# Turning attention weights with partition moves and VectorE in place of TensorE, in a one-core encoder block

## The reference

```python
# differential attention, 8 heads: 64-wide q and k in two maps, 128-wide v, 64-token chunks, block-causal
p = softmax(where(mask, q @ k.T * 64**-0.5, -inf))      # (8 heads, 2 maps, 256, 256)
a = p[:, :, 0] - lam * p[:, :, 1]
o = rmsnorm(a @ v, g_diff_sub) * (1.0 - lambda_init)    # per head, then @ w_diff_out

# cross attention into 256 memory tokens, 4 heads of width 256
s = (q @ k.T) * 256**-0.5
o = softmax(s) @ v                                      # then @ w_cross_out
merged = g_a * y_conv + g_b * y_diff + g_c * y_cross
```

## Time and profile before

| what | value |
|---|---|
| median of 3 runs | 1661.82 us (1661.12 to 1662.33) |
| the profiled execution's own time | 1663.99 us |
| its span in the trace | 1662.2 us |
| TensorE's granted clock, mean of the span | 0.999 of full speed |
| PE busy | 1648.3 us, 99% of the span, 7397 instructions |
| DVE busy | 991.1 us, 60%, 1259 instructions |
| ACT busy | 832.6 us, 50%, 1062 instructions |
| POOL busy | 23.6 us, 1% |
| DMA moved | 338.78 MB, mean 204 GB/s |

### The profile page before, as it was taken

The page is one execution under the profiler, slowest core; times in us unless marked ns, Lnnn a source line. Parts: engine busy times, 40 slices in busy tenths (PEclk is TensorE's granted clock), DMA queues, the critical chain, the costliest instruction groups (busy, mean ns, idle before and its releaser), DMA issues.

```text
span 1662.2 us, 22134 instructions
## 1 busy us (share of the span) xinstructions
PE 1648.3 (99%) x7397; PEld 1361.0 (82%) x7397; DVE 991.1 (60%) x1259; ACT 832.6 (50%) x1062; POOL 23.6 (1%) x53
## 2 busy tenths in 40 slices
PE   8999999999999999999999999999999999999998
PEld 7888888888888888888888888888888888888886
DVE  5555556655556656656555657676667767744544
ACT  5544444444444444444445556656666565543442
POOL 0000000000000000000000000000000000000000
PEclk9999999999999999999999999999999999999999
DMA  7677666777556655566556477777777777755653
GB/s 273 204 207 207 183 177 183 228 215 221 186 184 199 229 189 183 184 228 196 195 188 215 143 213 216 221 213 222 216 215 226 209 210 225 241 191 172 218 190 139
DMA packets 191907, 338.78 MB, mean 204 GB/s; under 512 B 19224, under 2 KB 37481, under 8 KB 191337
## 3 DMA queue, kind: packets, MB, share of 16 engines
q1 hardware_dynamic: 191817, 338.01, 64.9%
q10 hardware_dynamic: 32, 0.01, 0.0%
HBM read 318.02 MB, written 2.10 MB: 193 GB/s over the span
## 4 chain that ended last, share of the span: by engine, by line
PE 97%; DVE 1%; ACT 1%; issue 1%; DMA 0%; DVEq 0%; SPq 0%; POOL 0%; ACTq 0%; POOLq 0%
PE PS L1267 28%; PE PS L1269 28%; PE PS L1268 27%; PE PS L1414 3%; PE PS L1413 3%; PE PS L1412 3%; PE PS L1448 1%; PE PS L1447 1%; PE PS L1446 1%; PE PS L1281 1%; ACT w_hi L499 0%; PE PS L1353 0%; PE PS L1338 0%; DMA mem_sb<-in_mem_dram 0%; ACT p_diff L635 0%
## 5 line engine op out<-in xcount | busy, mean ns | idle before, releaser
L834 DVE TENSOR_TENSOR w_lo<-raw,w_hi 128x1024 fp32r<-128x1024 f32 x567 | 691.0, 1225 | 608.0 <-ACT w_hi L499 606.4
L499 ACT ACTIVATE w_hi<-raw 128x1024 fp32r<-128x1024 f32 x567 | 597.5, 1059 | 656.3 <-PE PS L1269 603.1
L1267 PE MATMUL PS<-w_hi,hT_hi 128*128 128x512 f32 x1504 | 590.0, 392 | 0.0
L1269 PE MATMUL PS<-w_hi,hT_lo 128*128 128x512 f32 x1504 | 585.6, 389 | 0.0
L1268 PE MATMUL PS<-w_lo,hT_hi 128*128 128x512 f32 x1504 | 585.3, 389 | 0.0
L1267 PEld LDWEIGHTS PS<-w_hi,hT_hi 128*128 128x128 f32 x1504 | 282.4, 188 | 60.4 <-issue 2.7
L1269 PEld LDWEIGHTS PS<-w_hi,hT_lo 128*128 128x128 f32 x1504 | 282.3, 188 | 58.9
L1268 PEld LDWEIGHTS PS<-w_lo,hT_hi 128*128 128x128 f32 x1504 | 282.5, 188 | 57.7
L1267 PE MATMUL PS<-w_hi,act_hi 128*128 128x512 f32 x336 | 130.9, 389 | 0.0
L1269 PE MATMUL PS<-w_hi,act_lo 128*128 128x512 f32 x336 | 130.7, 389 | 0.0
L1268 PE MATMUL PS<-w_lo,act_hi 128*128 128x512 f32 x336 | 130.7, 389 | 0.0
(11 more groups left out here) (217 smaller groups left out, 1269.7 us busy)
## 6 DMA issues: line engine op xcount, KB each, us to landing
raw<-in_w_up_dram SPq DMA_DIRECT2D x176, 512.0 KB, 4.0
raw<-in_w_in_dram SPq DMA_DIRECT2D x112, 512.0 KB, 4.1
raw<-in_w_gate_dram SPq DMA_DIRECT2D x96, 512.0 KB, 4.2
raw<-in_w_down_dram SPq DMA_DIRECT2D x88, 512.0 KB, 4.2
raw<-in_w_mem_kv_dram SPq DMA_DIRECT2D x32, 512.0 KB, 4.0
raw<-in_w_o_dram SPq DMA_DIRECT2D x32, 512.0 KB, 3.6
up_moved<-up_stage SPq DMA_DIRECT2D x352, 32.0 KB, 2.8
raw<-in_w_conv_out_dram SPq DMA_DIRECT2D x16, 512.0 KB, 3.7
```

The lines of the kernel that those rows point to most:

```text
L499: nc.scalar.activation(w_hi[i % RING][:], raw[i % RING][:], ACT.Copy).then_inc(hi_ready, inc)
L834: nc.vector.tensor_tensor(w_lo[i % RING][:], raw[i % RING][:], w_hi[i % RING][:].bitcast(F32), ALU.subtract).then_inc(lo_ready, inc)
L1267: nc.tensor.matmul(o, a_hi, b_hi, start=first, stop=False)
L1269: last = nc.tensor.matmul(o, a_lo, b_hi, start=False, stop=last_k)
```

## The change

- **Cross heads.** PE's four turns and ACT's copy are gone. DVE normalizes into `p_stage` in 32-wide squares (four instructions in place of two). SP moves the squares to `p_moved` with 16 DMAs of 32 partitions by 512 bytes, four behind each of the loads 4 to 7 of chunk `c = h + 8`. DVE turns them in four instructions behind its block 4 of that chunk. PE multiplies with the values behind block 2 of it, one chunk later than before, into another PSUM bank; ACT and DVE split the result behind 6.
- **Differential heads, weights.** PE's three turns and ACT's copy are gone. DVE writes `a_stage` in squares (three instructions in place of two). SP moves them to `a_moved` with 16 DMAs of 32 partitions by 384 bytes: behind loads 10 and 11 of the step and loads 0 and 1 of the next. DVE turns them in three instructions behind block 11, before the gate's argument. PE multiplies behind block 9 in place of 4. ACT's squares move behind block 0 of the next step, DVE's scaling behind its block 2.
- **Differential heads, outputs.** PE's two turns per head are gone. DVE scales into `o_stage`. Once for four heads, in step j = 0 of r = 1 and of r = 2, SP moves them with 16 DMAs of 32 partitions by 1 KB behind loads 6 to 9, DVE turns them in four instructions behind block 7, and ACT and DVE split four heads at once behind 8.
- **POOL.** The copy of the next head's q and k now comes ahead of the norm of the last head.

```diff
+        a_stage = at("a_stage", RD + 71 * K, [P, P // SQ, 3, SQ])
+        a_moved = at("a_moved", RD + 72 * K + 512, [P, P // SQ, 3, SQ])
+        a_diffT = at("a_diffT", RD + 74 * K, [P, 3 * P])
+        p_stage = at("p_stage", RD + 72 * K, [P, P // SQ, 2 * NT, SQ])
+        p_moved = at("p_moved", RD + 74 * K, [P, P // SQ, 2 * NT, SQ])
+        o_stage = at("o_stage", RD + 32 * K, [P, P // SQ, NCH, NT, SQ])
+        o_moved = at("o_moved", RB + 24 * K, [P, P // SQ, NCH * NT, SQ])
+        o_turned = at("o_turned", RB + 28 * K, [P, NCH, TOK])
...
+            def move_cross(h, a):
+
+                if a == 0:
+                    sp.wait_ge(x_norm, h + 1)
+                    if h:
+                        sp.wait_ge(x_pT, h)
+                for m in range(P // SQ):
+                    sp.dma_start(p_moved[SQ * m:SQ * (m + 1), a, :, :].rearrange("p q n -> p (q n)"),
+                                 p_stage[SQ * a:SQ * (a + 1), m, :, :].rearrange("p q n -> p (q n)")).then_inc(x_in_p, 16)
...
+            def move_diff(q, a):
+
+                if a == 0:
+                    sp.wait_ge(d_a, q + 1)
...
+                for m in range(P // SQ):
+                    sp.dma_start(a_moved[SQ * m:SQ * (m + 1), a, :, :].rearrange("p q n -> p (q n)"),
+                                 a_stage[SQ * a:SQ * (a + 1), m, :, :].rearrange("p q n -> p (q n)")).then_inc(d_a_in, 16)
...
+            def move_heads(half, a):
+
+                if a == 0:
+                    sp.wait_ge(d_on, NCH * (half + 1))
+                for m in range(P // SQ):
+                    sp.dma_start(o_moved[SQ * m:SQ * (m + 1), a, :, :].rearrange("p q n -> p (q n)"),
+                                 o_stage[SQ * a:SQ * (a + 1), m, :, :, :].rearrange("p h t n -> p (h t n)")).then_inc(d_o_in, 16)
...
+                    if 0 <= c - 1 - CROSS_STEP < CH and i >= CB - P // SQ:
+                        move_cross(c - 1 - CROSS_STEP, i - (CB - P // SQ))
...
+            def moves(r, j, q, i):
+
+                first = isinstance(j, int)
+                if i < 2 and not (first and r == 0) and (first or r < 2):
+                    move_diff(q - 1, 2 + i)
+                if first and r and 6 <= i < 6 + P // SQ:
+                    move_heads(r - 1, i - 6)
+                if r < 2 and i >= SB - 2:
+                    move_diff(q, i - (SB - 2))
...
+                    moves(r, j, q, i)
...
+                    moves(r, j, q, CB + i)
...
             with pool.Fori(1, DH) as h:
-                head(h)
+                head_rows(h)
+                head_norm(h - 1)
+            head_norm(DH - 1)
...
-                        if i == 7:
-                            act.wait_ge(x_pT, h + 1)
-                            nc.scalar.activation(p_crossT[:], PS[:, 7, :].rearrange("p (a b) -> p a b", a=NT), ACT.Copy).then_inc(x_pT_sb, 1)
-                        if i == 7:
-                            act.wait_ge(x_oT, h + 1)
-                            nc.scalar.activation(y_cross_hi[:, 2 * h:2 * h + 2, :],
-                                                 PS[:, 6, :].rearrange("p (a b) -> p a b", a=2), ACT.Copy).then_inc(x_hi, 1)
+                    h = c - CROSS_STEP - 1
+                    if 0 <= h < CH and i == 6:
+                        act.wait_ge(x_oT, h + 1)
+                        nc.scalar.activation(y_cross_hi[:, 2 * h:2 * h + 2, :],
+                                             PS[:, 7, :].rearrange("p (a b) -> p a b", a=2), ACT.Copy).then_inc(x_hi, 1)
...
+                    first = isinstance(j, int)
+                    if i == 0 and not (first and r == 0) and (first or r < 2):
+                        act.wait_ge(d_o, q)
+                        for t in range(NT):
+                            last = nc.scalar.activation(p_diff[:, t, 0:P], PS[:, 5, t * P:(t + 1) * P], ACT.Square,
+                                                        accum_out=sq_o[:, t:t + 1])
+                        last.then_inc(d_sq, 1)
+                    if i == 8 and first and r:
+                        act.wait_ge(d_oT, r)
+                        nc.scalar.activation(y_diff_hi[:, NCH * (r - 1):NCH * r, :], o_turned[:], ACT.Copy,
+                                             scale=g_sub[:, 0:1]).then_inc(d_hi, 1)
...
-                        if i == 7:
-                            act.wait_ge(d_aT, q + 1)
-                            nc.scalar.activation(a_diffT[:], PS[:, 4, 0:3 * P], ACT.Copy).then_inc(d_aT_sb, 1)
-                        if i == 8:
-                            act.wait_ge(d_o, q + 1)
...
-                        if i == 11:
-                            act.wait_ge(d_oT, q + 1)
-                            nc.scalar.activation(y_diff_hi[:, bass.ds(q, 1), :], PS[:, 4, 0:TOK].rearrange("p (a t) -> p a t", a=1), ACT.Copy,
...
+                                for kb in range(NT):
+                                    last = nc.vector.tensor_scalar(p_stage[:, :, NT * t + kb, :],
+                                                                   p_cross[:, t, kb * P:(kb + 1) * P].rearrange("p (m n) -> p m n", n=SQ),
+                                                                   inv_e[:, 0, t:t + 1], None, ALU.mult)
...
+                    h = c - CROSS_STEP - 1
+                    if 0 <= h < CH:
+                        if i == 4:
+                            dve.wait_ge(x_in_p, MOVED * (h + 1))
+                            if h:
+                                dve.wait_ge(x_oT, h)
+                            for t in range(NT):
+                                for kb in range(NT):
+                                    last = nc.vector.transpose(p_crossT[:, kb, t * P:(t + 1) * P].rearrange("p (a n) -> p a n", n=SQ),
+                                                               p_moved[:, :, NT * t + kb, :])
+                            last.then_inc(x_pT, 1)
+                        if i == 6:
                             dve.wait_ge(x_hi, h + 1)
...
+                    if i == 2 and rp is not None and rp < 2:
+                        dve.wait_ge(d_r, q)
+                        for t in range(NT):
+                            last = nc.vector.tensor_scalar(o_stage[:, :, bass.ds(jp, 1), t, :].rearrange("p m h n -> p m (h n)"),
+                                                           PS[:, 5, t * P:(t + 1) * P].rearrange("p (m n) -> p m n", n=SQ),
+                                                           r_o[:, t:t + 1], None, ALU.mult)
+                        last.then_inc(d_on, 1)
+                    if r and isinstance(j, int):
+                        if i == 7:
+                            dve.wait_ge(d_o_in, MOVED * r)
+                            for a in range(P // SQ):
+                                last = nc.vector.transpose(o_turned.rearrange("p h (t n) -> p (h t) n", t=NT)[:, :, SQ * a:SQ * (a + 1)], o_moved[:, a, :, :])
+                            last.then_inc(d_oT, 1)
+                        if i == 8:
+                            dve.wait_ge(d_hi, r)
+                            s = slice(NCH * (r - 1), NCH * r)
...
+                            for b, t in enumerate((0, 1, 1)):
+                                p0, p1 = (p_diff[:, m, b * P:(b + 1) * P].rearrange("p (m n) -> p m n", n=SQ) for m in range(2))
+                                last = nc.vector.scalar_tensor_tensor(out=a_stage[:, :, b, :], in0=p0, scalar=inv_e[:, t, 0:1], in1=p1,
+                                                                      op0=ALU.mult, op1=ALU.add)
                             last.then_inc(d_a, 1)
-                        if i == 9:
-                            dve.wait_ge(d_r, q + 1)
-                            for t in range(NT):
-                                last = nc.vector.tensor_scalar(o_diff[:, t, :], PS[:, 5, t * P:(t + 1) * P], r_o[:, t:t + 1], None, ALU.mult)
-                            last.then_inc(d_on, 1)
+                        if i == 11:
+                            dve.wait_ge(d_a_in, MOVED * (q + 1))
+                            if not (isinstance(q, int) and q == 0):
+                                dve.wait_ge(d_on, q)
+                            for b in range(3):
+                                last = nc.vector.transpose(a_diffT[:, b * P:(b + 1) * P].rearrange("p (a n) -> p a n", n=SQ), a_moved[:, :, b, :])
+                            last.then_inc(d_aT, 1)
...
-                    if r < 2 and i == 11:
-                        dve.wait_ge(d_hi, q + 1)
-                        nc.vector.scalar_tensor_tensor(out=y_diff_lo[:, bass.ds(q, 1), :].rearrange("p a t -> p (a t)"), in0=PS[:, 4, 0:TOK],
-                                                       scalar=g_sub[:, 0:1],
-                                                       in1=y_diff_hi[:, bass.ds(q, 1), :].bitcast(F32).rearrange("p a t -> p (a t)"),
-                                                       op0=ALU.mult, op1=ALU.subtract).then_inc(d_lo, 1)
...
-                        if i == 3:
```

(31 more changed lines are left out.)

44 lines of the change are left out of this document (17 added, 27 removed).

## The result

The changed kernel takes 1666.74 us (median of 12 runs, 1663.88 to 1669.55), the kernel before, run beside it, 1662.72 (12 runs, 1661.12 to 1663.78): a ratio of 1.0024, 95% interval 1.0016 to 1.0031. It is 0.24% slower, where the forecast was 1660.4 and no measurable difference. The number lies inside the range given, the sign was missed. The profiled execution took 1667.92 us.

The account below looks back on a forecast made before the run. PE's instruction list plus PE's waits was taken to bound the kernel: -9.05 (turns off PE) + 3.3 (cross waits) + 4.3 (differential waits) = -1.4 us, against the median of 1661.82 giving 1660.4 us; range 1655.5 to 1667.

Parts of the forecast that it names:

- What bounds the kernel.: Whole kernel: time is PE's instruction list plus PE's waits; work added to DVE, ACT or SP counts only through those waits.
- the rest, at nothing: Output moves of four heads, ACT's copies and later waits, POOL's norm, SP's late loads: together 0 us.
- The sum taken off PE, 9.05 us.: PE's list: removed turns save 1.96 us in cross heads, 5.09 for differential weights and 2.00 for differential outputs.
- Rival 3: PE's turns: part of their displacement is a refill other pieces also pay, so half of 9.05 us, 1664.9 us; chance 0.07.
- Four moves and their load repeat every 3.08 us.: SP's queue: each slot of one load and four moves takes 3.08 us, against 2.72 us for a block.
- Differential waits, 4.3 us.: PE behind block 9: no wait in r = 0, 0.5 to 1.4 us per step in r = 1, sum 4.3 us.
- Cross waits, 3.3 us.: PE before the cross value products: nothing in chunks 8 and 10, 1.0 us in chunk 9, 2.3 us in chunk 11.
- SP's moves land before the convolution ends in both: Chunks 9 and 11: the cross heads' moves land before DVE's convolution ends, so they add no wait.
- The landing, 2.7 us, and the turns, 0.9 and 0.7 us.: A slot's last move lands 2.7 us after issue; DVE's turns take 0.9 us for four, 0.7 for three.
- rival 2: Differential steps' fourth slot: weights' moves land 1.4 us later than counted, costing 10.8 us, so 1671.2 us; chance 0.18.

Follow-up runs that it names:

- run 6: Changed kernel with cross value products behind PE's block 4 (split behind 7) and the differential weights' moves one load earlier: 1655.64 us, ratio 0.9963.
- run 1: Changed kernel with only the cross heads on the new way; differential heads keep PE's turns and ACT's copies: 1664.92 us, ratio 1.0014.
- run 3: Changed kernel with the cross value products behind block 4 in place of 2, their split behind 7 in place of 6: 1661.56 us, ratio 0.9991.
- run 4: Changed kernel with 18 unused identity products put on PE in chunk 11 ahead of the wait for the last cross head: 1667.33 us, ratio 1.0027.
- run 5: Changed kernel with the differential weights' moves issued one load earlier on SP, cross heads as in the changed kernel: 1660.77 us, ratio 0.9991.
- run 2: Changed kernel with only the differential heads on the new way; the cross heads stay as before: 1663.92 us, ratio 1.0006.
- run 8: Kernel of run 6 with the cross value products back behind PE's block 2 in chunk 11 alone: 1659.38 us, ratio 0.998.

## Why the prediction was wrong, step by step

- **What bounds the kernel.** Right. PE's list, PE's waits and the clock account for 3.5 of the 4.0 us. PE waits for `w_lo` or `raw` nowhere new. But "the rest, at nothing" did not hold for the output moves of four heads: they made DVE stand 4.4 us in q4's step, and by the load that this held up they cost an estimated 0.9 us there.
- **The sum taken off PE, 9.05 us.** Right, to some hundredths (run 6). Rival 3 fell.
- **"Four moves and their load repeat every 3.08 us."** This step failed. The rows stood in a stretch that is written out and in which SP had no hitch. In the branches a slot within a step takes 3.08 to 3.2 us, but the one that crosses into the next step took 3.63, 3.76, 3.68, 3.08, 4.44, 3.53, 3.50 and 3.08 in q0 to q7, and in q0, q1 and q5 a single slow issue came on top. I had allowed 0.3 us for the loop's turn, with 0.6 as its bound, and nothing for the rest. The chain of four slots was 0.1 to 1.9 us longer in seven of eight heads. In the written-out code of the cross heads slow issues made it 1.1 to 1.5 us longer in three of four chunks.
- **Differential waits, 4.3 us.** Measured 6.6. r = 1 behind its first head was near by the sum (3.8 us forecast, 3.3 measured), with some luck: the forecast rose from 1.0 to 1.4 and 1.4, the waits were 1.3, 1.3 and 0.7, with longer chains and an earlier landing than assumed. r = 0 was put at none with 0.5 us to spare, and q0 and q1 waited 1.5 us; q4 was put at 0.5 and waited 1.9. All three had chains of 13.1 us and more. A margin of 0.5 us on a chain of twenty issues is no margin.
- **Cross waits, 3.3 us.** Measured 4.2, in the chunks and the order given: 1.08 for 1.0, 0.35 for nothing, 2.74 for 2.3. The convolution ahead of the turns was the main cause, as forecast. That "SP's moves land before the convolution ends in both" failed in chunk 11: behind the convolution DVE waited 0.4 us more for `p_moved`, whose slots had a slow issue. Chunk 10, put at nothing with 0.3 us to spare at least, has no convolution; its 0.35 us go with the slow issue that made its slots 1.1 us longer.

```profile
281.95 1.66 DVE L935 SCALAR_TENSOR_TENSOR convT<-proj_turned,vecs,convT 128x254 f32<-128x254 f32 x4
284.03 0.89 DVE L1036 STREAM_TRANSPOSE p_crossT<-p_moved 128x128 f32<-128x128 f32 x4 [0.42 <-DMA p_moved<-p_stage]
```

- **The landing, 2.7 us, and the turns, 0.9 and 0.7 us.** The turns were right (0.89 and 0.70). The landing was better than assumed: by the start of DVE's turns the last moves of the eight heads landed 1.9 to 2.5 us after their issue, and all moves of the weights had this spread:

```profile
DMA to landing us min/median/max: 1.8/2.5/4.6
```

The rule of the Trainium skill ("DMA: Bandwidth & Descriptors", Specifications) on transfers under 512 bytes did not show on these rows of 384 bytes: their median of 2.5 us is below the 3.0 of the 1-KB rows of `proj_moved` in the same profile. That agrees with the same page's remark (Why small descriptors are slow) that moves inside SBUF are spared, though these moves are also smaller as a whole, 12 KB for 32. So rival 2 came true in its outcome and part of its place, with waits in r = 0 as its sign, but not by its mechanism: the moves land early enough after their issue, they are issued late. That the measured time lies inside the stated range is owed to the room left for this rival.
- **The clock.** No term of the sum had it. I wrote of a wait of 2.3 us in chunk 11 and took it at its length. It cost 1.7 us more in the profile. Without it the kernel would still have been slower, by some 2.3 us where -1.4 was forecast: the waits by themselves (10.8 us for 7.6) turn the sign.
- The rule of the Trainium skill that speaks against the change ("VectorE: DVE Perf Modes", Rules for kernel authors: TensorE for a full 128x128 transpose) agrees with the changed kernel, at 1666.7 us, and not with run 6 at 1655.6, which turns the same blocks on VectorE. Where PE is 99% busy, what decides is whether the detour is started early enough.

In one line: -9.05 (right) + 4.2 (for 3.3) + 6.6 (for 4.3) + 1.7 (for nothing) = +3.5, and 0.5 us open.

## What to carry to other kernels

Work taken off the bounding engine pays only if its replacement is early by more than the spread of its chain, not by its mean: here, moving the consumer two blocks later and the moves one load earlier turned +4.0 us into -6.8. Take the price of a queue's slot from the same kind of code (written out, or across the turn of a loop) and count its hitches: here six of twelve chains of twenty issues met a slow one. Ask also what an engine off the critical path waits for: DVE's wait for the output moves came back to PE through a load. And price a wait of TensorE of two or three microseconds at up to twice its length: the clock fell in five of the seven profiles with waits of 1.9 us or more, at 1.7 to 2.7 us each.

## What the runs showed of the hardware

- The granted clock of TensorE fell to half at waits of 1.9 to 2.7 us, at some and not at others of the same length: at 2.6 (changed kernel), 2.3 (run 1), 2.7 (run 3), 1.9 (run 4) and 2.1 us (run 5), and not at 2.9 (run 2), 2.6 (run 8), 2.0 (run 4), 1.9 (run 5) and 1.7 us (changed kernel). In four profiles it fell 0.4 to 1.4 us after PE had resumed and stayed down for some 3.4 us; in run 3 it fell while PE stood and stayed down for nearly 7. What decides it stays open.
- The spread of the runs does not follow the waits alone. It is 5.7 us in the changed kernel, 6.5, 5.5 and 6.1 in runs 2, 3 and 4, but 3.0 and 1.9 in runs 1 and 5, which have waits of more than 2 us too, and 2.7 in the kernel before.
- A DMA issue on SP takes 0.59 us, and rarely up to 1.77 (of 128 moves of the weights); in the kernel before too there are single issues of this length, up to 2.1 us. What they wait for was not tried.
